# Another order of TensorE's steps in the four attention parts, as a table for each layer

## What is computed

```python
def first_block(x, ...):
    for l in range(DEPTH):                       # DEPTH = 2
        proj = x @ w_in[l]
        hq, hf, hi, hg, nq, kc, vc, ks, vs, kw, vw, gt = jnp.split(proj, pts, axis=-1)
        o_a = hgrn2_mixer(hq, hf, hi, hg, lbs[l], hg_norm_w[l])
        o_b = nsa_mixer(nq, kc, vc, ks, vs, kw, vw, gt, ...)
        mix = jnp.concatenate([o_a, o_b], axis=-1) @ w_out[l]
        x = layer_norm(ALPHA * x + mix, ln1_g[l], ln1_b[l])
        ffn = (jax.nn.silu(x @ w_ffn_gate[l]) * (x @ w_ffn_up[l])) @ w_ffn_down[l]
        x = layer_norm(ALPHA * x + ffn, ln2_g[l], ln2_b[l])
    return x

# compressed branch of nsa_mixer, per block of queries
s_c = jnp.einsum('bghtd,bgnd->bghtn', qblk, kc) * scale + head_bias(...)
p_c = masked_softmax(s_c, valid_c)
o_c = jnp.einsum('bghtn,bgnd->bghtd', p_c, vc)   # kc, vc = gelu(blocks @ w1) @ w2
```

```python
def second_block(x, ...):
    for layer in range(DEPTH):
        h = rmsnorm(x, attn_norm[layer])
        ...                                      # attention: `mixed`
        x = x + mixed @ w_o[layer]
        h = rmsnorm(x, ffn_norm[layer])
        x = x + conv_ffn(h, w_up[layer], conv_w[layer], conv_b[layer], w_down[layer])
    return rmsnorm(x, final_norm)
```

## Time and profile before

| | us |
|---|---|
| median of three runs | 1450.47 |
| their lowest and highest | 1443.47, 1452.86 |
| the profiled execution | 1455.39 |
| its span, first to last instruction | 1453.6 |
| TensorE's matmuls busy | 1391.5 |
| VectorE busy | 958.6 |
| ScalarE busy | 721.1 |
| GpSimd busy | 85.2 |
| TensorE's mean granted clock, share of full | 0.977 |

### The profile page before, as it was taken

One profiled execution on the slowest core, in us unless ns is written; L12 is line 12 of the kernel. 1 busy time (PEld: TensorE's weight loads), 2 busy tenths in 40 slices (PEclk: granted clock), 3 DMA queues, 4 the chain that ended last, 5 costly groups with the idle time before them and its releaser, 6 DMA issues.

```text
span 1453.6 us, 24532 instructions
## 1 busy us (share of the span) xinstructions
PE 1391.5 (96%) x10006; PEld 1288.2 (89%) x10006; DVE 958.6 (66%) x1630; ACT 721.1 (50%) x1199; POOL 85.2 (6%) x79
## 2 busy tenths in 40 slices
PE   9998999999998898999997999999999999999998
PEld 7997789999898777999997999889999999889997
DVE  5666675555759567655566686587777655687776
ACT  4755344343475623443334554555555544654554
POOL 0321000000005100000000003040000000000000
PEclk9999899999999988999999999999999999999999
DMA  8742145555353302755544334345555534445541
GB/s 315 279 154 87 59 145 203 175 191 186 132 216 117 116 30 87 238 197 174 189 160 159 117 117 138 140 169 182 189 189 174 188 117 145 151 158 201 200 176 58
DMA packets 38632, 233.22 MB, mean 160 GB/s; under 512 B 5017, under 2 KB 8809, under 8 KB 12153
## 3 DMA queue, kind: packets, MB, share of 16 engines
q1 hardware_dynamic: 36456, 224.18, 43.5%
q0 software_dynamic: 2064, 7.47, 1.6%
HBM read 230.55 MB, written 1.09 MB: 159 GB/s over the span
## 4 chain that ended last, share of the span: by engine, by line
PE 82%; DVE 9%; ACT 5%; issue 2%; DMA 1%; POOL 1%; SPq 0%; DVEq 0%; ACTq 0%
PE bank L770 20%; PE bank L771 19%; PE bank L772 19%; PE bank L778 4%; PE bank L779 4%; PE bank L782 4%; DVE w_lo L605 2%; PE bank L893 2%; PE bank L973 1%; ACT w_hi L595 1%; PE bank L995 1%; PE bank L997 1%; PE bank L996 1%; DVE arena L1711 1%; DMA arena<-in_w_idx 1%
## 5 line engine op out<-in xcount | busy, mean ns | idle before, releaser
L605 DVE TENSOR_TENSOR w_lo<-raw,w_hi 128x1024 fp32r<-128x1024 f32 x404 | 484.9, 1237 | 92.6 <-ACT w_hi L595 89.4
L770 PE MATMUL bank<-a_hi,w_hi 128*128 128x256 f32 x1856 | 530.5, 286 | 5.7 <-DVE w_lo L605 5.7
L771 PE MATMUL bank<-a_lo,w_hi 128*128 128x256 f32 x1856 | 526.2, 284 | 0.0
L772 PE MATMUL bank<-a_hi,w_lo 128*128 128x256 f32 x1856 | 526.1, 283 | 0.0
L595 ACT ACTIVATE w_hi<-raw 128x1024 fp32r<-128x1024 f32 x404 | 406.4, 1050 | 99.9 <-PE bank L772 66.0
L770 PEld LDWEIGHTS bank<-a_hi,w_hi 128*128 128x128 f32 x1856 | 357.0, 192 | 10.5 <-issue 7.5
L771 PEld LDWEIGHTS bank<-a_lo,w_hi 128*128 128x128 f32 x1856 | 357.2, 192 | 1.2
L772 PEld LDWEIGHTS bank<-a_hi,w_lo 128*128 128x128 f32 x1856 | 357.1, 192 | 0.0
L778 PE MATMUL bank<-w_hi,a_hi 128*128 128x256 f32 (+1 forms) x320 | 105.3, 349 | 8.3 <-ACT a_hi L621 7.0
L1711 DVE SCALAR_TENSOR_TENSOR arena<-bank,conv_col,arena 128x254 f32<-128x254 f32 (+1 forms) x176 | 76.7, 477 | 51.8 <-ACT arena L1294 50.1
L771 PE MATMUL bank<-w_lo,h_hi 128*128 128x512 f32 x264 | 105.2, 398 | 0.0
(11 more groups left out here) (264 smaller groups left out, 1967.9 us busy)
## 6 DMA issues: line engine op xcount, KB each, us to landing
raw<-in_stream SPq DMA_DIRECT2D x201, 1024.0 KB, 4.9
bias_t<-bias_rows SPq DMA_DIRECT2D x6, 512.0 KB, 6.7
heads_buf<-in_w SPq DMA_DIRECT2D x2, 1024.0 KB, 8.0
gains<-in_w SPq DMA_DIRECT2D x2, 1024.0 KB, 10.1
gains<-in_ln_g POOLq DMA_DIRECT2D x4, 512.0 KB, 4.1
gains<-in_ln_b POOLq DMA_DIRECT2D x4, 512.0 KB, 5.4
gains<-in_rms_g POOLq DMA_DIRECT2D x3, 512.0 KB, 4.0
res<-in_xT SPq DMA_DIRECT2D x4, 256.0 KB, 5.4
```

Of the source, the lines that this page charges most:

```text
L605: dve.tensor_tensor(w_lo[:, i % PARTS, half_tile(h)], raw[:, i % SLOTS, half_tile(h)], w_hi[:, i % PARTS, half_tile(h)].bitcast(F32), ALU. ...
L770: pe.matmul(out, lh, rh, start=first, stop=False)
L771: pe.matmul(out, lh, rl, start=False, stop=False)
L772: return pe.matmul(out, ll, rh, start=False, stop=last)
```

## The change

`plan` no longer puts its list together from pieces; it reads it from a table `STEPS`, one text for each layer. The helpers `halves` and `out` go. `woven` and everything else stay. Each layer's list has the same steps as before (95, 95, 89 and 61) in another order; `a` steps keep their order among themselves, so the stream of tiles is the same. The steps that change places:

- Layer 0: `gtT` before `hid 3`; `S 1` before `a nq1`; `oT 0` before `T 0`, and `out 0 0 0` behind `T 0`, both ahead of `phase out`; then `oT 1`, `S 2`, and `S 3` before `out 0 0 1`; `out 1 1 0` before `S 6`; `out 2 0 1` before `V 6`, `out 2 1 0` before `V 7`, `out 2 1 1` before `oT 3`.
- Layer 1: `gt` before `level 3`; `hid 1` before `b hg1`; `S 1` before `a nq1`; `oT 0` before `S 2`, `out 0 0 0` before `oT 1`; `cs` before `S 4`; `out 1 1 0` before `cT`; `out 1 1 1` before `co 1`; `T 7` before `V 6`.
- Layer 2: `I 1` before `b qi2`; `I 7` before `b k0`; `V 0` before `a k1`; `oT 1` behind `b v3`; `out 0 0 0` ahead of `phase out`; `phase out1` ahead of `oT 2`.
- Layer 3: `S 1` before `b q1`; `T 1` before `S 2`; `S 3` before `V 1`; `a v2` before `T 3`; `V 4` behind `a k3`, `V 5` behind `S 6`; `oT 2` before `out 1 0 1`; `phase out1` before `T 7`.

```diff
@@ -67,10 +67,6 @@
 HEAD_TILES = {0: ["hi0", "hi1"], 1: ["hi0", "hi1"], 2: ["v0", "v1"], 3: ["v0", "v1"]}
 
 
-def halves(*names):
-    return [(half, name) for name in names for half in ("a", "b")]
-
-
 def woven(steps):
 
 
@@ -89,52 +85,46 @@
     return out + highs + lows
 
 
-def out(r, tt):
-    return [("out", r, tt, hf) for hf in range(2)]
+
+
+STEPS = {
+    0: """
+        a hf0, b hf0, a hf1, b hf1, a hq0, gates, b hq0, logs, a hq1, sums, b hq1, a kskw, decay 1, b kskw,
+        decay 2, a nq0, level 0, b nq0, level 1, a kcvc, level 2, b kcvc, level 3, a hg0, level 4, b hg0,
+        level 5, gt, a hg1, level 6, hid 0, b hg1, level 7, hid 1, a vsvw, silu, level 8, hid 2, phase
+        heads, ho 0, ho 1, b vsvw, gtT, hid 3, S 0, hidT, S 1, a nq1, ho_out, kcv, b nq1, oT 0, T 0, out 0 0
+        0, phase out, oT 1, S 2, V 0, T 1, S 3, out 0 0 1, V 1, out 1 0 0, T 2, S 4, phase out1, out 1 0 1,
+        V 2, cs, T 3, out 0 1 0, S 5, V 3, out 0 1 1, T 4, cT, out 1 1 0, S 6, V 4, T 5, co 0, co 1, out 1 1
+        1, oT 2, S 7, V 5, T 6, out 2 0 0, out 2 0 1, V 6, T 7, out 2 1 0, V 7, out 2 1 1, oT 3""",
+    1: """
+        a hf0, b hf0, a hf1, b hf1, a hq0, gates, b hq0, logs, a hq1, b hq1, sums, a kskw, b kskw, decay 1,
+        a nq0, decay 2, b nq0, level 0, a kcvc, level 1, b kcvc, level 2, a hg0, gt, level 3, b hg0, level
+        4, a hg1, level 5, level 6, hid 0, hid 1, b hg1, level 7, a vsvw, silu, level 8, hid 2, phase heads,
+        ho 0, ho 1, b vsvw, hid 3, gtT, S 0, hidT, S 1, a nq1, ho_out, kcv, b nq1, T 0, phase out, oT 0, S
+        2, out 0 0 0, oT 1, V 0, T 1, out 0 0 1, S 3, V 1, out 1 0 0, T 2, cs, S 4, phase out1, out 1 0 1, V
+        2, T 3, out 0 1 0, S 5, V 3, out 0 1 1, T 4, out 1 1 0, cT, S 6, V 4, T 5, co 0, out 1 1 1, co 1, oT
+        2, S 7, V 5, T 6, out 2 0 0, T 7, V 6, out 2 0 1, V 7, out 2 1 0, oT 3, out 2 1 1""",
+    2: """
+        phase tiles, kw, a qi0, b qi0, kwT, a qi1, b qi1, kiT, a qi2, I 0, I 1, b qi2, a qi3, I 2, b qi3, I
+        3, a q0, I 4, b q0, I 5, a k0, I 6, I 7, b k0, S 0, a q1, choose 0 2, b q1, T 0, choose 0 2, S 1, V
+        0, a k1, choose 0 2, b k1, T 1, choose 0 2, S 2, a q2, V 1, choose 1 2, b q2, T 2, choose 1 2, S 3,
+        a k2, V 2, choose 1 2, b k2, choose 1 2, unsel, T 3, a v2, S 4, V 3, b v2, T 4, a q3, S 5, V 4, b
+        q3, T 5, a k3, V 5, oT 0, b k3, a v3, S 6, b v3, oT 1, out 0 0 0, phase out, out 0 0 1, T 6, S 7,
+        out 1 0 0, out 1 0 1, V 6, phase out1, oT 2, T 7, out 0 1 0, out 0 1 1, V 7, out 1 1 0, out 1 1 1,
+        oT 3, out 2 0 0, out 2 0 1""",
+    3: """
+        phase tiles, a q0, b q0, a k0, b k0, S 0, a q1, S 1, b q1, T 0, a k1, V 0, b k1, T 1, S 2, a q2, S
+        3, V 1, b q2, T 2, a k2, V 2, b k2, a v2, T 3, S 4, V 3, b v2, T 4, a q3, S 5, b q3, T 5, a k3, V 4,
+        oT 0, b k3, a v3, S 6, V 5, oT 1, b v3, phase out, out 0 0 0, out 0 0 1, T 6, S 7, out 1 0 0, oT 2,
+        out 1 0 1, V 6, phase out1, T 7, out 0 1 0, out 0 1 1, V 7, out 1 1 0, out 1 1 1, oT 3, out 2 0 0,
+        out 2 0 1""",
+}
 
 
 def plan(l):
 
-
-    if l < 2:
-        lead = halves("hf0", "hf1") + [("a", "hq0"), ("gates",), ("b", "hq0"), ("logs",), ("a", "hq1")]
-        if l == 0:
-            levels = ([("sums",), ("b", "hq1"), ("a", "kskw"), ("decay", 1), ("b", "kskw"), ("decay", 2)]
-                      + [("a", "nq0"), ("level", 0), ("b", "nq0"), ("level", 1), ("a", "kcvc"), ("level", 2), ("b", "kcvc")]
-                      + [("level", 3), ("a", "hg0"), ("level", 4), ("b", "hg0"), ("level", 5), ("gt",), ("a", "hg1")])
-        else:
-            levels = ([("b", "hq1"), ("sums",), ("a", "kskw"), ("b", "kskw"), ("decay", 1), ("a", "nq0"), ("decay", 2)]
-                      + [("b", "nq0"), ("level", 0), ("a", "kcvc"), ("level", 1), ("b", "kcvc"), ("level", 2)]
-                      + [("a", "hg0"), ("level", 3), ("b", "hg0"), ("level", 4), ("gt",), ("a", "hg1"), ("level", 5)])
-        levels += ([("level", 6), ("hid", 0), ("b", "hg1"), ("level", 7), ("hid", 1), ("a", "vsvw"), ("silu",)]
-                   + [("level", 8), ("hid", 2), ("phase", "heads"), ("ho", 0), ("ho", 1)])
-        return woven(lead + levels + [("b", "vsvw"), ("hid", 3), ("gtT",), ("S", 0), ("hidT",), ("a", "nq1"), ("S", 1), ("ho_out",)]
-                     + [("kcv",), ("b", "nq1"), ("T", 0), ("phase", "out"), ("S", 2), ("oT", 0), ("oT", 1), ("out", 0, 0, 0)]
-                     + [("V", 0), ("T", 1), ("out", 0, 0, 1), ("S", 3), ("V", 1), ("out", 1, 0, 0), ("T", 2), ("S", 4)]
-                     + [("phase", "out1"), ("out", 1, 0, 1), ("V", 2), ("cs",), ("T", 3), ("out", 0, 1, 0)]
-                     + [("S", 5), ("V", 3), ("out", 0, 1, 1), ("T", 4), ("cT",), ("S", 6), ("out", 1, 1, 0), ("V", 4)]
-                     + [("T", 5), ("co", 0), ("co", 1), ("out", 1, 1, 1), ("oT", 2), ("S", 7), ("V", 5), ("T", 6)]
-                     + [("out", 2, 0, 0), ("V", 6), ("T", 7), ("out", 2, 0, 1), ("V", 7), ("out", 2, 1, 0), ("oT", 3)]
-                     + [("out", 2, 1, 1)])
-    if l == 2:
-        lead = ([("kw",)] + halves("qi0") + [("kwT",)] + halves("qi1") + [("kiT",)]
-                + [("a", "qi2"), ("I", 0), ("b", "qi2"), ("I", 1), ("a", "qi3"), ("I", 2), ("b", "qi3"), ("I", 3)]
-                + [("a", "q0"), ("I", 4), ("b", "q0"), ("I", 5), ("a", "k0"), ("I", 6), ("b", "k0"), ("I", 7)]
-                + [("S", 0), ("a", "q1"), ("choose", 0, 2), ("b", "q1"), ("T", 0), ("choose", 0, 2), ("S", 1)]
-                + [("a", "k1"), ("V", 0), ("choose", 0, 2), ("b", "k1"), ("T", 1), ("choose", 0, 2), ("S", 2)]
-                + [("a", "q2"), ("V", 1), ("choose", 1, 2), ("b", "q2"), ("T", 2), ("choose", 1, 2), ("S", 3)]
-                + [("a", "k2"), ("V", 2), ("choose", 1, 2), ("b", "k2"), ("choose", 1, 2), ("unsel",), ("T", 3)])
-    else:
-        lead = (halves("q0", "k0")
-                + [("S", 0), ("a", "q1"), ("b", "q1"), ("S", 1), ("T", 0)]
-                + [("a", "k1"), ("V", 0), ("b", "k1"), ("S", 2), ("T", 1)]
-                + [("a", "q2"), ("V", 1), ("b", "q2"), ("S", 3), ("T", 2)]
-                + [("a", "k2"), ("V", 2), ("b", "k2"), ("T", 3)])
-    return woven([("phase", "tiles")] + lead
-                 + [("a", "v2"), ("S", 4), ("V", 3), ("b", "v2"), ("T", 4), ("a", "q3"), ("S", 5), ("V", 4), ("b", "q3")]
-                 + [("T", 5), ("a", "k3"), ("V", 5), ("oT", 0), ("b", "k3"), ("a", "v3"), ("S", 6), ("oT", 1), ("b", "v3")]
-                 + [("phase", "out")] + out(0, 0) + [("T", 6), ("S", 7)] + out(1, 0) + [("V", 6), ("oT", 2), ("T", 7)]
-                 + [("phase", "out1")] + out(0, 1) + [("V", 7)] + out(1, 1) + [("oT", 3)] + out(2, 0))
+    steps = [step.split() for step in STEPS[l].split(",")]
+    return woven([tuple(int(x) if x.isdigit() else x for x in step) for step in steps])
 
 
 def rest(l):
```

## The result

The changed kernel takes 1433.6 us (median of 6 executions, 1429.7 to 1434.8), the kernel before 1449.5 us (6 executions, 1443.5 to 1452.9): a ratio of 0.989, 95% interval 0.986 to 0.991. The forecast was 1434 us, in a range of 1427 to 1446.

A forecast was written before the change was run, and what follows sets the result against it. TensorE, busy 96% of the span, was taken as the bound. Idle time -7.3 us and clock -11.1 us made -18.4 us on 1455.4 us; some 16.5 us off the 1450.5 us median gave 1434 us, range 1427 to 1446.

The forecast's parts named there:

- part b: First output product, layers 0 and 1: idle time -1.5 and -2.2 us, low-clock stretches gone, -1.7 us each.
- a: Compression's hidden layer, layers 0 and 1: 1.90 us waits split but kept, 0 us; layer 1's low stretch gone, -1.7 us.
- rival 3: Slower: clock falls at places with new waits while old falls stay, 1.7 us each, at seven 1455 us; chance 0.03.
- c: Compressed softmax, layer 1, cs two steps earlier: idle time -0.95 us, clock -3.45 us.
- rival 4: More than forecast: layer 0's low stretch to 153.19 shortens too and (c) keeps none, 1428 us; chance 0.13.
- d: Before S 6, layers 0 and 1: out 1 1 0 covers the 0.66 us wait in both, -1.3 us.
- e: Layer 1, co 1 behind out 1 1 1: oT 2 loses its cover, +0.9 us.
- f: End of attention: layer 0 idle time -0.55 us, clock -1.7 us; layer 1 idle time -0.5 us, clock -0.85 us.
- g: Layer 2: S 0 +0.75 us, oT 1 -0.45 us, out 0 1 0 -0.75 us; sum -0.45 us.
- h: Layer 3: T 1 before S 2, -0.75 us; V 4's queueing 0; T 5's bound 0 to +1.
- rival 1: Idle time goes, but the clock falls at as many places: only -7.3 us, 1443 us; chance 0.24.
- Rival 2: Gain given back as waits one step on, about a fifth left: 1448 us; chance 0.10.

The follow-up runs named there:

- filled runs: Extra matmuls put into TensorE's pauses: in the kernel before 1441.3 us, in the order of e1_s1_behind 1430.1 us, in that of e8 1429.1 us.
- e8: Order of e1_s1_behind with cs (layer 0) ahead of S 4, co 1 (layer 1) ahead of out 1 1 1, I 7 behind b k0: 1428.9 us.
- e7_first_product: Kernel before with only oT 0 and the first output product moved ahead in layers 0 and 1: 1444.4 us, 0.9958 of the kernel before.
- e3_cs_behind: Changed kernel with cs of layer 1 moved back behind V 2, its place before the change: 1435.2 us.
- e1_s1_behind: Changed kernel with S 1 moved back behind a nq1 in layers 0 and 1: 1434.2 us.
- e4_layer1_alone: Kernel before with the new table for layer 1 only: 1441.6 us.
- e11_layer0_alone: Kernel before with the new table for layer 0 only: 1442.4 us.
- the filled kernel: Kernel before in its old order, with extra matmuls put into TensorE's pauses: 1441.3 us.

## Why the prediction came out right, and where it did not

The total was right: 15.9 us by the medians of the two sixes, 17.3 us against the 45 executions, 16.5 forecast, 1433.6 against 1434. By the averages the columns also come near the terms: the clock's part 27.7 to 16.7 is -11.0 us, the rest 1421.0 to 1414.2 is -6.8 us. But the forecast's -11.1 and -7.3 were made for the profiled execution, and there, by the clocks of 0.977 and 0.986, the clock's part fell by 13.4 us and the rest by 7.3: 20.7 us for 18.4. The step from the profiled 18.4 to 16.5 against the median was taken from the total and from neither column. It was in the right direction (the profiled pair lies 20.7 us apart, the medians 17.3); that -11.0 meets -11.1 is in part luck.

**The step that does not hold by itself is the price of a low stretch.** The sum took half of 3.41 us for each, everywhere. The filled runs show that this is its price only where no wait follows. Of 20.3 us of clock's part 9.6 us were time in the old order (some 11 without the late V 6), of 10.5 us 4.1 in the new one, of 7.8 us none in e8. The idle terms were too small by the other side of the same error: they were read from waits that the low clock had shortened (1.6 us before S 5 of layer 1, 2.57 us behind full clock in e7_first_product and e3_cs_behind; in layer 0, where no term was taken, 1.13 and 2.2 us). Held at full clock the order is worth some 10 us, not 7.3; what goes through the clock is then about 7 us, not 11. The two errors are two sides of one, and so the total came out: part b, alone in e7_first_product, gave 3.4 and 3.2 us for terms of 3.7 and 3.4.

Term by term:
- **a.** The waits stay and are split, as said: 0.93 + 0.81 us in layer 0, 1.75 us in layer 1, for 1.90 each. The clock was wrong: the stretch in layer 1 did not go but doubled (482.16 to 488.99), and layer 0 got one at 113.52. S 1 had been taken for cover that could be spared because a projection half followed the pause; but that half had been the work between the pauses. This is rival 3's mechanism at two of its places, and e1_s1_behind shows that it cost nothing in the end.
- **b.** Waits of 1.12 us and 0.44 + 0.69 us where 0.85 and 0.95 us were forecast (the prediction does not say from which rows the 0.95 comes). Both low stretches are gone; the old order has them at this place in the other traces too (e4_layer1_alone in layer 0, e11_layer0_alone in layer 1). e7_first_product measured it alone: 6.1 to 6.5 us for 7.1.
- **c.** The wait before S 5 went (0.16 left), 0.45 us came before out 0 1 0 (forecast 0.65). But undoing it cost 1.6 to 2.4 us and not 4.4: as far as the overlapping executions tell, the clock's 3.45 us was the mis-sized term. With cs in its old place again one stretch of 3.41 us came, so the old 10.24 us at 0.50 were not the place of cs alone. In layer 0, where cs stayed, they shrank to 3.41 as well, as rival 4 has it; but they are 3.41 us in e4_layer1_alone too, whose layer 0 is not changed, so this is not shown to be the change's doing.
- **d.** Both waits of 0.66 us before S 6 are gone.
- **e.** 1.05 us before oT 2, forecast 0.9.
- **f.** Layer 0 has 0.22 us before V 6 and 0.99 before out 3 0 0 (forecast 0 and 1.0), layer 1 has 0.81 us before T 7 (forecast 1.1), and both low stretches are gone; of these, the one of layer 0 is missing from the unchanged layer 0 of e4_layer1_alone too. Not forecast: the wait at the next normalization fell from 2.92 to 1.96 us in layer 0.
- **g, h.** Layer 2: 0.73 us before S 0 (forecast 0.75), 0.25 before the first product for 0.69 (forecast -0.45), none before out 0 1 0. Layer 3: no wait before S 2 that the timeline shows. In the feed-forward part behind layer 2 0.6 us came back, not forecast: TensorE's wait for h_hi is 2.15 us for 1.52. These were seen in the traces only; no run measured layers 2 and 3 alone.

Of the rivals, 1 fell by the time and by the clock's part, 27.7 to 16.7 us on average; the clock of 0.96 and 0.94 in the two stretches would not do it alone, since the unchanged layer 0 of e4_layer1_alone has 0.94. The Trainium skill ("TensorE: Matmul & The Clock Gate", section "A second HAM failure mode: psum-queue depth-cycling") names short pauses between groups of matmuls as what makes the clock go back and forth; the filled kernel bears that out, since the clock stays up when the pauses are filled (27.7 to 7.4 us). What the prediction drew from it for rival 1, that shorter pauses would cost as much clock, did not come. Rival 2, that the gain is given back one step on, holds for single steps (kcv, I 7, T 3) and not for the whole; its time should have been 1447 us and not 1448, since a fifth of 16.5 is 3.3 us.

## What to carry to other kernels

A stretch at the low clock is worth half its length only if TensorE's work from there on is never waited out by another engine's chain; follow the work to the next wait before you price it, and expect that wait to grow. When a wait vanishes from one step look for it in the sum over its chain: moving steps around the chain on ScalarE left about 3 us in three orders, while starting the chain earlier (oT 0 ahead of S 2, cs ahead of S 4) really shortened it. In a table with rotating PSUM banks, a moved step can also turn the ring for later layers. And where the same order shows 0.88 and 0.94 in two executions, do not price a low stretch from one of them.
